# FFN input projection as seven half-size block products per tile pair, with a float32 hidden result and a down projection that walks the depth

## The chip, the cores and the metric

The kernel runs on one core of a Trainium2 chip. The metric is device time in microseconds (us). Five engines of the core work side by side and are ordered only by semaphores: TensorE (PE) multiplies, VectorE (DVE), ScalarE (ACT) and GpSimd (POOL) do the element work, and SyncE (SP) issues the DMAs.

## The reference, cut to what matters

Two transformer-like blocks are computed on a sequence of 512 tokens of width 1024. The change touches only the feed-forward part of the first block:

```python
hffn = modulate(rmsnorm(x, g_norm2[l]), shift2, scale2)
a, u = jnp.split(jnp.einsum('bsd,df->bsf', hffn, w_ffn_in[l]), 2, axis=-1)   # f = 2 * 2816
x = x + gate2[:, None, :] * jnp.einsum('bsf,fd->bsd', jax.nn.silu(a) * u, w_ffn_out[l])
```

All of it is float32. The kernel keeps this precision on PE by splitting each operand into a rounded high part (type F32R) and the remainder, the low part; a product is three matmuls: high times high, high times low, low times high.

## The kernel before, in words

Activations lie with the features on the 128 partitions and the 512 tokens along the free axis. The weights come as a stream of units, 128 x 1024 float32 (512 KB): one unit holds the 8 depth blocks of one output tile of 128 features. Each unit passes a ring of 4 slots: SP loads it into `raw` (`load`, L452), ACT writes the high part `w_hi` (`split_hi`, L598), POOL writes the low part `w_lo` = raw - w_hi (`split_lo`, L534), PE uses it and adds to `unit_used`. `split_hi(u)` waits until unit u-4 has been used, `load(u)` until the low part of unit u-4 is made. The streams of the engines are written out by hand, and each engine works its own stream in order.

The norm ahead of the projection is made in two halves of 256 tokens (HALF): DVE writes the normed half to `tn`, ACT the high part `x_hi`, DVE the low part `x_lo` (`normed_half`, `hi_half`, `low_half`). PE works tile pair 0 (units 0 and 1 of "ff_in") half by half as they come, then units 2 and 3 at full width into PSUM banks of `aux`.

There are 22 tile pairs, a gate tile and an up tile each, 44 units. From pair 2 on PE runs `tiles("ff_in", ...)` (L2470), which calls `tile` (L2117): a tile is 8 depth blocks x 3 matmuls = 24 matmuls of 512 columns, 48 for a pair. For each pair ACT makes silu of the gate tile (`ff_pair`, L833), DVE multiplies it with the up tile out of PSUM into `ht` (`ff_product`, L1517, the product in L1520), ACT writes the high part `h_hi` and DVE the low part `h_lo` (L1524). These two hold the whole hidden result, 22 tiles.

The down projection (`down`, L2472) makes the 8 output tiles one after the other, 22 depth blocks x 3 matmuls each, 528 in all; an output is done every 15 us or so. After each, DVE adds it to `resid` (L1544), ACT writes the high part of the next stage's operand (`next_hi`), DVE its low part (L1559) and sums of squares (L1548 to L1556). The next stage, "gdn_in", starts with depth blocks 0 to 3 of its first tile, then four matmuls for the norm's sums (`two_stats`, L2509 to L2512) that wait for the squares of the last output, then blocks 4 to 7.

Of the kernel before, what the change touches and what calls it, by code (L numbers as in the profile page):

```python
# [33 lines left out]
F32 = mybir.dt.float32  # L34
F32R = mybir.dt.float32r
# [91 lines left out]
def loop(eng, n, counts):  # L127
# [15 lines left out]
    ("ff_in", 44), ("ff_out", 24),  # L143
# [4 lines left out]
    ("first", 182), ("gdn_in", 25), ("mix_out", 6), ("kv", 8), ("xq", 8), ("x_val", 8), ("xo", 4),  # L148
# [6 lines left out]
Q_AT, V_AT = (0, 1, 2, 3, 4, 5, 8, 9), (6, 7, 10, 11, 12, 13, 14, 15)  # L155
LEVELS = 7
# [52 lines left out]
def build_program(nc, dram):  # L209
    ctx = ExitStack()  # L210
    with ctx:
# [46 lines left out]
        def overlay(start, *specs):  # L258
# [44 lines left out]
        (ht, h_hi, h_lo), _ = overlay(  # L303
            over, ("ht", (P, 2, T), F32), ("h_hi", (P, FT, T), F32R), ("h_lo", (P, FT, T), F32R))
# [91 lines left out]
        def sem(name):  # L396
# [54 lines left out]
        def _(sp_):  # L451
# [39 lines left out]
            def load_units(first, end):  # L491
                with sp_.Fori(0, (end - first) // 4) as i:
                    for j in range(4):
                        load(At(first + j, i, 4))

# [20 lines left out]
            load_units(rest, U0["mix_out"] + 4)  # L516
# [16 lines left out]
        def _(pool):  # L533
# [13 lines left out]
            split_units(U0["sb_qk"], U0["gdn_in"])  # L547
# [43 lines left out]
        def _(act):  # L591
# [150 lines left out]
            with loop(act, RET_H, [(own["rv_ready"], 4), (own["tile_done"], 8), (own["oraw_ready"], 4),  # L742
                                   (own["stat_ready"], 1), (own["root_ready"], 1), (own["gate_ready"], 4),
                                   (own["oprod_ready"], 4), (own["orh_ready"], 4)]) as i:
# [13 lines left out]
                def product_hi(e):  # L758
                    own["oprod_ready"].next()
                    own["orh_ready"].own(f(orh[:, e, :], oraw[:, e, :]))  # L760
# [19 lines left out]
            for n in range(KT):  # L780
# [6 lines left out]
                own["merged_f"].next()  # L787
                own["merged_hi"].own(f(m_hi[:, n, :], mt[:, n % 2, :]))
# [13 lines left out]
            def hi_half(k, c):  # L802
                own["normed"].next()
                own["norm_hi"].own(f(x_hi[:, k, c], tn[:, k % 2, c], ACT.Identity,
                                     bias=mod[:, 3 * KT + k:3 * KT + k + 1]))
# [27 lines left out]
            def ff_pair(k, u, n, gate_bank, freed):  # L833
                split_hi(u + AHEAD)
                act.wait_ge(unit_used, (u + 1).val())
                own["gate_ready"].own(f(gate_t[:, n, :], gate_bank, ACT.Silu))
                if freed is not None:
                    nc.scalar.sem_inc(acc_free[freed], 1)
                split_hi(u + 1 + AHEAD)
                own["hidden_f"].next()  # L840
                own["hidden_hi"].own(f(h_hi[:, bass.ds(k, 1), :].rearrange("p a n -> p (a n)"), ht[:, n, :]))

            ff_pair(0, At(U0["ff_in"]), 0, bank(At(0)), 0)
            ff_pair(1, At(U0["ff_in"] + 2), 1, aux[:, T:2 * T], None)
            with loop(act, FT // 2 - 1, [(own["gate_ready"], 2), (own["hidden_f"], 2), (own["hidden_hi"], 2)]) as i:
                for n in range(2):
                    ff_pair(i * 2 + (2 + n), At(U0["ff_in"] + 4 + 2 * n, i, 4), n, bank(At(2 * n)), 0)
            next_hi = {3: 0, 6: 1, 9: 2, 12: 3, 15: 4, 18: 5, 21: 6, 23: 7}
            for j in range(24):
                split_hi(At(U0["ff_out"] + j + AHEAD))  # L850
                if j == 8:
                    own["nega_ready"].own(f(nega[0:GDN_H, 0:1], cols[0:GDN_H, C0["a_log"]:C0["a_log"] + 1], ACT.Exp))
                    nc.scalar.preload_act_table_set("natural_log_exp_and_others")
                if j in next_hi:
                    k = next_hi[j]
                    own["res_ready"].next()
                    own["norm_hi"].own(f(x_hi[:, k, :], resid[:, k, :], scale=gain1[:, k:k + 1]))
# [245 lines left out]
            own["tile_done"].skip(6)  # L1103
# [46 lines left out]
            def hidden_half(n):  # L1150
                own["conv2_ready"].next()
                own["hidden_f"].next()
                own["hidden_hi"].own(f(at_tile(g_hi, n), ht2[:]))
# [15 lines left out]
            with loop(act, FT // 2 - 2, [(own["scaled"], 4), (own["conv0_ready"], 4), (own["conv2_ready"], 4),  # L1169
                                         (own["silu2_ready"], 2), (own["hidden_f"], 2), (own["hidden_hi"], 2)]) as i:  # L1170
# [26 lines left out]
        def _(dve):  # L1197
# [154 lines left out]
            for n in range(PAIRS):  # L1352
                own["gate_ready"].next()
                dve.wait_ge(unit_used, U0["sb_out"] + n + 1)
                own["msb_ready"].own(V.tensor_tensor(msb[:, n, :], sb_bank(n), gates[:, n, :], ALU.mult))
# [37 lines left out]
            with loop(dve, RET_H, [(own["recip_ready"], 1), (own["rs_ready"], 1), (step, 10 + 3 + 6 + 1 + 1 + 16), (own["qk_rot"], 2), (own["ada_used"], 8), (own["ada1_loaded"], 16 * KT),  # L1393
                                   (own["rsc_done"], 1), (own["rsc_ready"], 1), (own["decay_free"], 1),
                                   (own["oraw_ready"], 4), (own["sq_ready"], 1), (own["root_ready"], 1),
                                   (own["gate_ready"], 4), (own["oprod_ready"], 4), (own["orh_ready"], 4),
                                   (own["or_ready"], 4), (own["ada_ready"], 1), (own["tile_done"], 8)]) as i:
# [16 lines left out]
                for e in range(RET_VT):  # L1414
                    own["gate_ready"].next()
                    own["oprod_ready"].own(V.tensor_tensor(oraw[:, e, :], oraw[:, e, :], gate_t[:, e % 2, :], ALU.mult))
                    own["orh_ready"].next()
                    own["or_ready"].own(V.tensor_tensor(orl[:, e, :], oraw[:, e, :], orh[:, e, :].bitcast(F32),
# [1760 lines left out]
```

## Time and profile before

| | us |
|---|---|
| three runs | 2072.86, 2067.62, 2068.59 |
| median | 2068.59 |
| the profiled execution, first to last instruction (span) | 2066.4 |
| ff_in pairs 2 to 21 in it (868.93 to 1086.56) | 217.63 |
| down projection in it (1086.56 to 1207.43) | 120.87 |

Only the span is given for the profiled execution; it lies 2.2 us below the median of the three runs, which count some start and end of the program as well. In the profile, PE is matmul, PEld its weight load, DVE, ACT and POOL the three others. A matmul's recorded duration overlaps the next one, so its price is the distance from one start to the next. "idle ... <-X" is time in which an engine stood still until X let it go on.

### The profile page before, as it was taken

The numbers are of one execution on the slowest core, as the hardware profiler recorded it, in microseconds if no ns is written. First come the engines' busy times: TensorE is split into PE (matmuls) and PEld (weight loads), VectorE is DVE, ScalarE is ACT, GpSimd is POOL, SyncE is SP. The second block draws the span as 40 slices with busy tenths as digits, with TensorE's granted clock in tenths as the row PEclk, the third lists the DMA queues.
The fourth block names the chain that finished last, engine by engine and source line by source line (L and its number), as shares of the span: only waits on it lengthen the run. The fifth ranks groups of instructions, "written<-read, shape, count | busy, mean of one in ns | idle before, by whom it ended". The sixth has DMA issues, their size and how long they took to land.

```text
span 2066.4 us, 29038 instructions
## 1 busy us (share of the span) xinstructions
PE 2027.5 (98%) x10614; PEld 1653.1 (80%) x10614; DVE 915.2 (44%) x1175; ACT 890.3 (43%) x1103; POOL 898.8 (43%) x412
## 2 busy tenths in 40 slices
PE   9999999999999999999999999988999999999999
PEld 5888878787878788888888887767898778888887
DVE  4354434354545454511113346875671267555312
ACT  4476652323232333433232247678653335444321
POOL 3232234342424244444444546768355134444453
PEclk9999999999999999999999999999999999999999
DMA  8121223434333333233333332220244123333331
GB/s 333 60 63 60 62 77 112 143 107 141 108 134 115 132 95 99 82 92 101 94 99 97 107 96 69 81 62 3 83 142 128 35 82 101 93 95 98 101 103 61
DMA packets 56387, 203.84 MB, mean 99 GB/s; under 512 B 6256, under 2 KB 8432, under 8 KB 54896
## 3 DMA queue, kind: packets, MB, share of 16 engines
q1 hardware_dynamic: 56304, 202.70, 30.2%
q8 instruction: 57, 0.93, 0.2%
q14 instruction: 26, 0.21, 0.0%
HBM read 200.57 MB, written 2.10 MB: 98 GB/s over the span
## 4 chain that ended last, share of the span: by engine, by line
PE 75%; issue 8%; DVE 6%; POOL 4%; ACT 4%; DMA 1%; POOLq 0%; DVEq 0%; SPq 0%; ACTq 0%
PE acc L2089 18%; PE acc L2091 17%; PE acc L2090 17%; PE aux L2089 4%; PE aux L2091 4%; PE aux L2090 4%; POOL w_lo L537 3%; PE acc L2393 2%; POOL cfy L562 1%; DVE qkvf L1747 1%; PE aux L2291 1%; DMA ada<-in_ada 1%; PE aux L2286 1%; DVE cfy L1670 1%; PE aux L2304 1%
## 5 line engine op out<-in xcount | busy, mean ns | idle before, releaser
L537 POOL TENSOR_TENSOR w_lo<-raw,w_hi 128x1024 fp32r<-128x1024 f32 x317 | 775.0, 2450 | 1111.8 <-ACT w_hi L596 1110.9
L596 ACT ACTIVATE w_hi<-raw 128x1024 fp32r<-128x1024 f32 x317 | 335.3, 1061 | 541.9 <-PE acc L2091 400.6
L2089 PE MATMUL acc<-x_hi,w_hi 128*128 128x512 f32 (+1 forms) x1336 | 523.3, 392 | 9.6 <-DVEq L1207 4.0
L2091 PE MATMUL acc<-x_hi,w_lo 128*128 128x512 f32 (+1 forms) x1336 | 516.7, 387 | 0.0
L2090 PE MATMUL acc<-x_lo,w_hi 128*128 128x512 f32 (+1 forms) x1336 | 516.5, 387 | 0.0
L2089 PEld LDWEIGHTS acc<-x_hi,w_hi 128*128 128x128 f32 x1336 | 250.9, 188 | 65.9 <-DVEq L1207 6.0
L2091 PEld LDWEIGHTS acc<-x_hi,w_lo 128*128 128x128 f32 x1336 | 250.8, 188 | 51.8
L2090 PEld LDWEIGHTS acc<-x_lo,w_hi 128*128 128x128 f32 x1336 | 251.0, 188 | 49.7 <-issue 0.5
L1520 DVE TENSOR_TENSOR ht<-acc,tn 128x512 f32<-128x512 f32 x21 | 14.5, 692 | 173.8 <-PE acc L2091 171.3
L1249 DVE SCALAR_TENSOR_TENSOR adac<-ada,c_act,adac 128x1024 f32<-128x1024 f32 x28 | 40.4, 1444 | 92.7 <-DMA ada<-in_ada 92.2
L562 POOL TENSOR_TENSOR cfy<-cfy,tn 128x512 f32<-128x512 f32 x51 | 70.0, 1373 | 21.7 <-ACT tn L596 19.1
L2089 PE MATMUL aux<-x_hi,w_hi 128*128 128x512 f32 x192 | 74.9, 390 | 0.8 <-POOL w_lo L537 0.8
L2090 PE MATMUL aux<-x_lo,w_hi 128*128 128x512 f32 x192 | 74.7, 389 | 0.0
L2091 PE MATMUL aux<-x_hi,w_lo 128*128 128x512 f32 x192 | 74.7, 389 | 0.0
L2089 PE MATMUL acc<-h_hi,w_hi 128*128 128x512 f32 x176 | 69.3, 394 | 0.0
L2091 PE MATMUL acc<-h_hi,w_lo 128*128 128x512 f32 x176 | 69.0, 392 | 0.0
L2090 PE MATMUL acc<-h_lo,w_hi 128*128 128x512 f32 x176 | 68.3, 388 | 0.0
L2089 PE MATMUL aux<-w_hi,x_hi 128*128 128x512 f32 x160 | 63.7, 398 | 0.7 <-DVE x_lo L1279 0.7
L2091 PE MATMUL aux<-w_hi,x_lo 128*128 128x512 f32 x160 | 62.4, 390 | 0.0
L2090 PE MATMUL aux<-w_lo,x_hi 128*128 128x512 f32 x160 | 62.3, 389 | 0.0
L596 ACT ACTIVATE tn<-acc 128x512 f32<-128x512 f32 x37 | 22.1, 597 | 84.2 <-PE acc L2091 84.2
L2089 PE MATMUL acc<-g_hi,w_hi 128*128 128x512 f32 (+1 forms) x154 | 58.1, 378 | 0.0
(536 smaller groups left out, 3573.2 us busy)
## 6 DMA issues: line engine op xcount, KB each, us to landing
raw<-in_weights SPq DMA_DIRECT2D x324, 512.0 KB, 3.6
ada<-in_ada SPq DMA_DIRECT2D x32, 512.0 KB, 3.6
ada<-in_ada_first SPq DMA_DIRECT2D x8, 1024.0 KB, 12.3
resid<-in_x SPq DMA_DIRECT2D x2, 1024.0 KB, 6.2
out<-resid SPq DMA_DIRECT2D x16, 128.0 KB, 1.8
decay<-in_tables SPq DMA_DIRECT2D x4, 256.0 KB, 3.6
memf<-in_mem SPq DMA_DIRECT2D x1, 1024.0 KB, 4.9
angles<-in_tables SPq DMA_DIRECT2D x1, 512.0 KB, 5.2
```

The source lines that it names most:

```text
L537: nc.gpsimd.tensor_tensor(lo_home(u), raw[s][:], hi_home(u).bitcast(F32), ALU.subtract).then_inc(lo_ready, 1)
L562: tap_used.own(nc.gpsimd.tensor_tensor(cfy[:, n, :], cfy[:, n, :], product(tap_used.at.c), ALU.add))
L596: return nc.scalar.activation(out, in_, func, **kw)
L1249: return V.scalar_tensor_tensor(dst[:], w, c, dst[:], ALU.mult, ALU.add)
L1670: ins = V.scalar_tensor_tensor(y, x, w, y, ALU.mult, ALU.add)
L1747: ins = V.scalar_tensor_tensor(y[:, d:], bank(t)[:, 0:T - d], w, y[:, d:], ALU.mult, ALU.add)
L2089: M(out, a_hi, b_hi, start=first, stop=False)
L2090: M(out, a_hi, b_lo, start=False, stop=False)
L2091: return M(out, a_lo, b_hi, start=False, stop=last)
L2286: M(zp[h][:, a + w - v:a + w], negone_r[:], part[:, b:b + v], start=False, stop=False, skip_group_check=True)
L2291: m = M(zp[h][:, a:end], negtri_r[:], part[:, a:end], start=False, stop=part is sp_lo[h], skip_group_check=True)
L2393: m = M(bank(t)[:, j * P:T], rv[:, j, e * P:(e + 1) * P], rsc[:, a:a + w], start=j == 0, stop=j == NB - 1)
```

## The change

For pairs 2 to 21 (FAST = 2 pairs stay as they were), the product of a pair is one level of the Strassen-Winograd scheme. The weight's four blocks are (gate or up) x (first or second half of the depth), the activation's four are (half of the depth) x (half of the tokens). Seven products of 512 deep x 256 tokens take the place of eight: 7 x 4 depth blocks x 3 = 84 matmuls of 256 columns a pair instead of 48 of 512.

The scheme needs sums of blocks. For the activations they are made once, from a float32 copy `xf` of the normed input: three go to `t_hi`, `t_lo`, the fourth replaces a quarter of `x_hi`, `x_lo`. For the weights they are made for each pair: DVE forms four sums of 128 x 512 out of `raw` (`first_sums`, `last_sums`), one of them in place of a part of the raw unit; ACT writes their high parts (`split_sums`), DVE one low part (`sum_low`) and POOL another of 128 x 1024. The products' sums are added by DVE (`middle`, `ending`). The hidden result stays in float32 (`hf`).

The down projection goes through the depth with four output tiles at once, twice; the last 6 depth blocks of the second pass go output by output. The hidden tiles are split into high and low parts (`down_hi`, `down_low`) in a ring of 12, twice each. "ff_out" has 22 units instead of 24. Semaphores are merged and renamed to make room. The core of the diff:

```diff
 # stream of SP
+            load_units(rest, ff0 + 8)
+            for n in range(FT - FAST):
+                sp_.wait_ge(S["pair_made"], n + 1)
+                load(At(ff0 + 8 + 2 * n))
+                load(At(ff0 + 9 + 2 * n))
 # stream of POOL, for each pair
+                    split_lo(u)
+                    split_lo(u + 1)
+                    sums_hi.next()
+                    nc.gpsimd.tensor_tensor(wc_lo[n][:, T:3 * T], sum24[:], wc_hi[n][:, T:3 * T].bitcast(F32),
+                                            ALU.subtract).then_inc(sums_lo, 1)
 # stream of ACT
+            def split_diff(u):
+                own["sum_made"].next()
+                split_hi(u)
+            def split_sums(j, n):
+                if j is not None:
+                    act.wait_ge(S["tile_done"], j.val())
+                own["sum_hi"].own(f(wc_hi[n][:, 0:T], sum1[n]))
+                own["pair_made"].next()
+                own["pair_hi"].own(f(wc_hi[n][:, T:3 * T], sum24[:]))
...
+            with loop(act, (FT - FAST) // 2 - 1, [(own["sum_made"], 2), (own["logits_ready"], 2), (own["gate_ready"], 2),
...
                 for n in range(2):
+                    u = At(ff0 + 2 * FAST + 4 + 2 * n, i, 4)
+                    first_product(n)
+                    split_hi(u)
+                    split_diff(u + 1)
+                    fast_gate(n)
+                    split_sums(At(done + 4 * n + 4, i, 8), n)
...
+            for j in range(4, 22):
+                while made < min(2 * j + 6, 2 * FT):
+                    down_hi(made)
+                    made += 1
+                split_hi(At(U0["ff_out"] + j))
+                if j in (12, 14, 16, 18):
+                    next_hi((j - 12) // 2)
+            for j in range(3):
+                split_hi(At(U0["gdn_in"] + j))
+            for k in range(4, KT):
+                next_hi(k)
 # stream of DVE
+            def first_sums(u, n):
+                a, b = raw[u.slot(RING)], raw[(u + 1).slot(RING)]
...
+                step.own(V.tensor_tensor(sum1[n], b[:, 0:T], b[:, T:2 * T], ALU.add))
+                own["sum_made"].own(V.tensor_tensor(b[:, 0:T], a[:, 0:T], b[:, 0:T], ALU.subtract))
+            def last_sums(u, n, again=True):
+                a = raw[u.slot(RING)]
+                if again:
+                    own["pair_split"].next()
+                step.own(V.tensor_tensor(sum24[:, 0:T], sum1[n], a[:, 0:T], ALU.subtract))
+                own["pair_made"].own(V.tensor_tensor(sum24[:, T:2 * T], a[:, T:2 * T], sum24[:, 0:T], ALU.subtract))
+            def operand_low(n):
...
+                own["sum_hi"].next()
+                own["sum_split"].own(V.tensor_tensor(out, xf[:, k:k + HALF_K, c], hi.bitcast(F32), ALU.subtract))
...
+            first_sums(At(ff0 + 4), 0)
+            step.own(V.tensor_tensor(c_act[:, 0:HALF_K], mod[:, 3 * KT + HALF_K:4 * KT], mod[:, 3 * KT:3 * KT + HALF_K],
+                                     ALU.subtract))
+            for k in range(HALF_K):
+                r = xf[:, HALF_K + k, h1]
+                (step if k < HALF_K - 1 else own["sum_made"]).own(
+                    V.scalar_tensor_tensor(r, r, c_act[:, k:k + 1], xf[:, k, h1], ALU.add, ALU.subtract))
+            step.own(V.tensor_tensor(xf[:, 0:HALF_K, h1], xf[:, 0:HALF_K, h1], xf[:, 0:HALF_K, h0], ALU.subtract))
+            for k in range(HALF_K):
+                r = xf[:, k, h0]
+                (step if k < HALF_K - 1 else own["sum_made"]).own(
+                    V.scalar_tensor_tensor(r, r, shift[k], xf[:, HALF_K + k, h1], ALU.add, ALU.add))
+            for k in range(HALF_K):
+                r = xf[:, HALF_K + k, h0]
+                (step if k < HALF_K - 1 else own["sum_made"]).own(
+                    V.scalar_tensor_tensor(r, r, shift[HALF_K + k], xf[:, k, h0], ALU.add, ALU.subtract))
+            last_sums(At(ff0 + 4), 0, again=False)
+            hidden(0, bank(At(1)), gate_t[:, 0, :])
+            for n in range(3):
+                operand_low(n)
+            sum_low(0)
+            operand_low(3)
+            hidden(1, aux[:, 2 * T:3 * T], gate_t[:, 0, :])
+            first_sums(At(ff0 + 6), 1)
+            last_sums(At(ff0 + 6), 1)
+            sum_low(1)
+            def middle(n, k):
...
+                own["bank_free"].own(V.tensor_tensor(parts[:, h0], parts[:, h0], c[:, h0], ALU.add))
+                step.own(V.tensor_tensor(parts[:, h1], parts[:, h0], c[:, h1], ALU.add))
+                own["tile_done"].next()
+                own["bank_free"].own(V.tensor_tensor(
+                    hf[:, bass.ds(k, 1), :].rearrange("p a (b n) -> p (a b) n", b=2),
+                    parts[:, h1].rearrange("p (a n) -> p a n", a=1).broadcast_to([P, 2, T // 2]),
+                    b.rearrange("p (a n) -> p a n", a=2), ALU.add))
+            def ending(n, k):
+                own["tile_done"].next()
+                own["logits_ready"].own(V.tensor_tensor(a[:, h1], parts[:, h0], b[:, h1], ALU.add))
+                hidden(k, at_tile(hf, k), a)
+            with loop(dve, (FT - FAST) // 2 - 1, [(step, 6), (own["oraw_ready"], 2), (own["sum_made"], 2), (own["pair_split"], 2), (own["pair_made"], 2),
...
                 for n in range(2):
+                    u = At(ff0 + 2 * FAST + 4 + 2 * n, i, 4)
+                    first_sums(u, n)
+                    middle(n, i * 2 + (FAST + n))
+                    last_sums(u, n)
+                    ending(n, i * 2 + (FAST + n))
+                    sum_low(n)
...
+            for n in range(4, KT):
+                down_tile(n)
+                down_x(n)
+                if n < KT - 1:
+                    down_squares(n)
 # stream of PE
+            own["sum_split"].next(3)
+            own["sum_split"].skip()
+            with loop(pe, (FT - FAST) // 2, [(own["pair_split"], 2), (own["sum_split"], 2), (own["bank_free"], 4)]) as i:
                 for n in range(2):
+                    pe.wait_ge(S["tile_f"], At(made + 1 + n, i, 2).val())
+                    wa = weights(u)
+                    product(a[:, h0], *wa, 0, "b11", first=True).then_inc(S["tile_done"], 1)
+                    wb = weights(u + 1)
+                    product(c[:, h1], *wb, 0, "t3", first=True)
+                    product(b[:, h0], *wb, 1, "t4", first=True)
+                    own["pair_split"].next()
+                    product(c[:, h0], wc_hi[n], wc_lo[n], 1, "t2").then_inc(S["tile_done"], 1)
+                    own["sum_split"].next()
+                    product(b[:, h1], wc_hi[n], wc_lo[n], 0, "t1").then_inc(S["tile_done"], 1)
+                    own["bank_free"].next()
+                    product(a[:, h0], *wa, 1, "b21").then_inc(unit_used, 2)
+                    own["bank_free"].next()
+                    product(b[:, h1], wc_hi[n], wc_lo[n], 2, "b22").then_inc(S["tile_done"], 1)
```

`product` is 4 depth blocks x 3 matmuls of 256 columns. `hidden` multiplies with silu of the gate tile, `first_product` copies half of the first product out of PSUM, and both loops of ACT and DVE run over 18 of the 20 pairs, 2 at a time. `operand_low` writes a low part of 128 x 1024.

## Rows read from the trace of the kernel before

**Rows 1.** The page: the span, and PE's busy time.

```profile
span 2066.4 us, 29038 instructions
...
PE 2027.5 (98%) x10614; PEld 1653.1 (80%) x10614; DVE 915.2 (44%) x1175; ACT 890.3 (43%) x1103; POOL 898.8 (43%) x412
```

**Rows 2.** Windows: stretch, its length, then busy us (instructions) by engine, PE clock.

```profile
868.93:1086.56 217.63, 217.63 (x961) 180.24 (x960) 27.71 (x40) 67.08 (x80) 95.77 (x40) 1.00 0.31 97
1086.56:1207.43 120.87, 120.87 (x529) 99.16 (x528) 40.84 (x40) 31.97 (x34) 56.23 (x23) 1.00 0.33 101
```

**Rows 3.** Timeline of PE (start, us): first and last of 93 matmuls, 256 columns.

```profile
817.11 0.28 PE L2089 MATMUL aux<-m_hi,w_hi 128*128 128x256 f32 x1
...
827.94 0.28 PE L2091 MATMUL aux<-m_hi,w_lo 128*128 128x256 f32 x1
```

**Rows 4.** Groups by form, DVE, 780 to 1215: busy, mean ns, idle before.

```profile
L1524 DVE TENSOR_TENSOR h_lo<-ht,h_hi 128x512 f32 x20 | 13.9, 694 | 18.6 <-ACT h_hi L596 18.6
L1487 DVE SCALAR_TENSOR_TENSOR tn<-resid,gain,aux 128x256 f32<-128x256 f32 x16 | 7.7, 481 | 1.0 <-ACT aux L596 0.5
...
L1544 DVE SCALAR_TENSOR_TENSOR resid<-acc,mod,resid 128x512 f32<-128x512 f32 x8 | 6.0, 751 | 70.2 <-PE acc L2091 70.2
```

**Rows 5.** Groups by form, ACT, 780 to 1215.

```profile
L596 ACT ACTIVATE w_hi<-raw 128x1024 fp32r<-128x1024 f32 x79 | 83.6, 1060 | 115.3 <-PE acc L2091 103.3 <-ACT h_hi L596 4.4 <-ACT tn L596 4.3
L596 ACT ACTIVATE h_hi<-ht 128x512 f32 x20 | 12.6, 632 | 88.1 <-DVE ht L1520 88.1
...
L596 ACT ACTIVATE x_hi<-resid,gain 128x512 fp32r<-128x512 f32 x8 | 5.7, 707 | 0.0
```

**Rows 6.** Instructions of one line: duration ns min/median/max, first and last start.

```profile
L537 POOL TENSOR_TENSOR w_lo<-raw,w_hi x41: 2389/2394/2400, 866.0 to 1083.2; 128x1024 fp32r<-128x1024 f32 x41
...
L1831 DVE TENSOR_TENSOR xm<-xm,aux x20: 420/420/423, 1385.9 to 1421.3; 128x256 f32<-128x256 f32 x20
...
L1326 DVE TENSOR_TENSOR sp_lo<-sp,sp_hi x16: 1491/1493/1792, 97.9 to 284.5; 128x1280 fp32r<-128x1280 f32 x16
```

**Rows 7.** Timelines of POOL and DVE in the down projection.

```profile
1115.44 2.42 POOL L537 TENSOR_TENSOR w_lo<-raw,w_hi 128x1024 fp32r<-128x1024 f32 x1 [3.06 <-ACT w_hi L596]
1120.93 2.42 POOL L537 TENSOR_TENSOR w_lo<-raw,w_hi 128x1024 fp32r<-128x1024 f32 x1 [3.08 <-ACT w_hi L596]
...
1117.06 0.75 DVE L1544 SCALAR_TENSOR_TENSOR resid<-acc,mod,resid 128x512 f32<-128x512 f32 x1 [9.64 <-PE acc L2091]
...
1121.57 2.33 DVE L1559 SCALAR_TENSOR_TENSOR x_lo<-resid,gain,x_hi 128x512 fp32r<-128x512 f32 x1 [1.40 <-ACT x_hi L596]
```

**Rows 8.** Timelines of DVE and POOL, 101 to 108.

```profile
102.31 1.72 DVE L1326 TENSOR_TENSOR sp_lo<-sp,sp_hi 128x1280 fp32r<-128x1280 f32 x1 [0.68 <-ACT sp_hi L596]
104.06 2.51 DVE L1296 COPY spare<-v_sb 128x512 f32<-128x512 f32 x1
...
103.44 2.84 POOL L537 TENSOR_TENSOR w_lo<-raw,w_hi 128x1024 fp32r<-128x1024 f32 x1 [0.76 <-ACT w_hi L596]
```

**Rows 9.** Timelines of DVE and POOL where the change's setup begins.

```profile
856.65 0.48 DVE L1492 SCALAR_TENSOR_TENSOR x_lo<-tn,mod,x_hi 128x256 fp32r<-128x256 f32 x1 [0.19 <-ACT x_hi L596]
...
857.72 2.40 POOL L537 TENSOR_TENSOR w_lo<-raw,w_hi 128x1024 fp32r<-128x1024 f32 x1 [9.99 <-ACT w_hi L596]
```

**Rows 10.** Timelines of PE and DVE at the end of the down projection.

```profile
1207.43 0.40 PE L2089 MATMUL acc<-x_hi,w_hi 128*128 128x512 f32 x1
...
1210.20 1.02 PE L2509 MATMUL aux<-spare,two_sums 128*128 128x512 f32 x2
...
1207.70 0.75 DVE L1544 SCALAR_TENSOR_TENSOR resid<-acc,mod,resid 128x512 f32<-128x512 f32 x1 [6.89 <-PE acc L2091]
```

**Rows 11.** Windows, as Rows 2, around the clock's fall.

```profile
1421.80:1424.40 2.60, 0.51 (x16) 0.38 (x9) 1.18 (x2) 2.41 (x7) 2.44 (x3) 1.00 0.00 0
1425.00:1435.00 10.00, 8.77 (x74) 8.24 (x70) 5.48 (x10) 7.36 (x11) 9.45 (x8) 0.50 0.01 3
```

**Rows 12.** Timeline of PE: a gap without a fall.

```profile
1351.10 0.50 PE L2089 MATMUL acc<-x_hi,w_hi 128*128 128x512 f32 x1 [2.51 <-DVEq L1207]
```

More of the change, by code:

```diff
@@ L843, in _ @@
-            ff_pair(0, At(U0["ff_in"]), 0, bank(At(0)), 0)
-            ff_pair(1, At(U0["ff_in"] + 2), 1, aux[:, T:2 * T], None)
-            with loop(act, FT // 2 - 1, [(own["gate_ready"], 2), (own["hidden_f"], 2), (own["hidden_hi"], 2)]) as i:
-                for n in range(2):
[L847 to L857, printed above, removed]
+            ff0 = U0["ff_in"]
@@ new lines, in _ @@
+            first_product(0)
+            split_hi(At(U0["ff_out"]))
+            split_hi(At(U0["ff_out"] + 1))
+            fast_gate(0)
+            first_product(1)
+            for x in range(3):
+                down_hi(x)
+            split_hi(At(U0["ff_out"] + 2))
+            split_hi(At(U0["ff_out"] + 3))
+            fast_gate(1)
+            for x in range(3, 10):
+                down_hi(x)
+            own["nega_ready"].own(f(nega[0:GDN_H, 0:1], cols[0:GDN_H, C0["a_log"]:C0["a_log"] + 1], ACT.Exp))
@@ L2412, in _ @@
                 for e in range(RET_VT):
[L2413 removed]
+                    own["tile_split"].next()
                     project(0, e)
@@ new lines, in product @@
+            def product(out, wh, wl, at_, name, first=False):
+                hi, lo = operand(name)
+                for k in range(HALF_K):
+                    a = slice(at_ * T + k * P, at_ * T + (k + 1) * P)
+                    M(out, wh[:, a], hi[:, k, :], start=first and k == 0, stop=False, skip_group_check=True)
+                    M(out, wh[:, a], lo[:, k, :], start=False, stop=False, skip_group_check=True)
+                    m = M(out, wl[:, a], hi[:, k, :], start=False, stop=k == HALF_K - 1, skip_group_check=True)
+                return m
@@ new lines, in _ @@
+            d0 = U0["ff_out"]
+            for r in range(2):
+                for k in range(FT if r == 0 else FT - 6):
+                    x = r * FT + k
+                    own["tile_split"].next()
+                    if k % 2 == 0:
+                        wh, wl = weights(At(d0 + 11 * r + k // 2))
+                    for n in range(4):
+                        m = down_part(x, 4 * r + n, wh, wl, k % 2 * 4 + n, k == FT - 1, used=n == 1 and x > 0)
+                        if k % 2 and n == 3:
+                            m.then_inc(unit_used, 1)
+                        elif k == FT - 1:
+                            m.then_inc(S["tile_done"], 1)
@@ L3006, in _ @@
                         if n == 0 and k >= FT - 2:
-                            own["hidden"].next()
+                            own["tile_split"].next()
                         at_ = n % 4 * FT + k
```

328 lines of the change are left out of this document (226 added, 102 removed).

## The prediction

> **What bounds the kernel now.** I read the page first: PE is busy for 2027.5 of 2066.4 us, every other engine under half of it [rows 1]. So time can only be won by giving PE less, and any new wait of PE is lost time. The windows say what the stage touched is worth: pairs 2 to 21 take 217.63 us with PE never idle, 960 matmuls of 512 columns, so 226.7 ns each and 10.88 us a pair; POOL is busy for 96 us of it, DVE for 28. The down projection takes 120.87 us for 528 matmuls, also without a gap [rows 2]. Next I looked for matmuls of 256 columns, because the change lives by them: 93 stand in a row in the output projection, 92 distances in 10.83 us, 117.7 ns each, with waits that are already met between them [rows 3]. Last, and this decides the forecast, I compared the timelines of DVE and POOL. POOL's low part takes 2.39 us alone [rows 6]. A DVE operation with a PSUM operand runs through beside it in its usual 0.75 us. One whose two inputs both lie in SBUF started at 1121.57 while POOL ran to 1123.35 and ended at 1123.90: it stood still until POOL was done and took 0.55 us more [rows 7]. It works the other way too. POOL, called at 103.44 during such a DVE operation, took 2.84 us, and the next DVE operation, called 0.03 us after the first had ended, waited 2.2 us for POOL [rows 8]: whoever already waits goes first, so the two take turns.
>
> The Trainium skill states this as a rule ("SBUF — State Buffer", section "Who interferes with whom"): the port pair that DVE and GpSimd share is an exclusive lock, taken by a DVE instruction with two SBUF inputs against a GpSimd instruction that reads SBUF, and the loser waits. The trace agrees, by the rows named. It speaks against this change.
>
> **The pair, what PE gains.** 84 matmuls x 117.7 ns = 9.89 us instead of 10.88, so 0.99 us a pair and 19.8 us for 20 pairs. That is all the change can win. (The Trainium skill, "TensorE: Matmul & The Clock Gate", section "Wait — 56ns, not 53.3ns?", gives columns divided by 2.4 GHz plus 2.5 ns; by it a pair would go from 10.35 to 9.17 us, a gain of 1.18. The trace shows about 11 ns on top in place of 2.5, and I go by the trace.)
>
> **The pair, what is laid on the others.** POOL gets three operations of 1024 columns instead of two: 3 x 2.39 = 7.2 us. ACT gets three of 1.06, two of about 0.6 and a copy, 4.8 us [rows 5], no limit. DVE gets ten: five with a PSUM operand, which no one disturbs (0.42 us for 256 columns [rows 6], 0.69 for 512 [rows 4]), and five with both inputs in SBUF (`first_sums` 2, `last_sums` 2, `sum_low` 1), which share the lock with POOL: 0.69 us each, 0.55 after a wait. Together the lock is held 7.2 + 5 x 0.55 to 0.69 = 10.0 to 10.6 us a pair, already more than PE's 9.89. The order makes it worse, since one of these operations stands ahead of what PE waits for.
>
> I walk one pair j of the loop, from time 0, the end of the pair before. Hand-offs are 0.1 to 0.3 us (DVE starts 0.27 us after the nominal end of the last matmul [rows 10]). ACT's `split_hi` could start when product b21 of the pair before was done, at -1.2, and ends at -0.1. POOL: first low part 0 to 2.4. DVE adds the last product (0.2 to 0.6), ACT makes silu behind its second weight split (to 1.6) and the high part of the sum (to 2.3), DVE multiplies (to 2.45). `sum_low` is called at 2.5, when POOL has just started its second low part (2.3 to 4.7), and ends at 5.25. POOL's third, called since about 3.5, goes 5.2 to 7.55. `first_sums` is called at 5.3, between them: its first half waits to 7.55 and ends at 8.1, its second runs 8.15 to 8.85. Only then does DVE reach `middle`, whose data were there at 5.9 (four products, 5.65 us): 8.9 to 9.3. PE finished its fifth product at 7.06 and waits for `bank_free` until 9.45. The two products left end at 12.3; the other two additions of `middle` fit beside the sixth. So a pair takes 12.3 us, not 9.9: 1.42 us more than before, although PE works less. If `sum_low` gets in before the second low part, the same walk gives 12.1. `last_sums` falls into POOL's pause (10.6 to 12.1) and costs nothing, and the loads have over 5 us of air.
>
> **The first pairs.** Operand sums and splits stand between the last `low_half` (ends at 857.13 [rows 9]) and the third product, and PE waits for three of them before pair 2 begins, which before began at 868.93. DVE's list: two sums of 512 (1.4), a tiny one, 12 of 256 columns at 0.48 plus the gap between two [rows 4], one of 1024, two of 512, `hidden(0)` 0.7, three low parts of 1024. For 1024 columns I take 1.22, on the line between 0.69 at 512 and 1.49 at 1280 [rows 4, 6]. Alone that is 15.1 us, to 872.2, so 3.3 us of waiting. But POOL has five operations in this stretch (low parts of units 3 to 6 and the new one), and nearly all of DVE's are of the locked kind. Taking turns: unit 3 from 857.9 to 860.3 makes the second sum end at 860.85; units 4 and 5 follow, the first `xf` sum ends at 866.1, the chain of `xf` sums at 873.2, `hidden(0)` at 875.4, then low part, POOL, low part, POOL, low part: 876.7, 880.2, 883.6. PE starts pair 2 at 883.75: +14.8 us. Behind this DVE still has `sum_low(0)`, the fourth low part, `hidden(1)`, four sums for pair 3, `sum_low(1)` and the sums for pair 4 before `middle` of pair 2, with POOL twice between: `middle` starts at 895.8 and pair 2 ends at 899.2, 15.45 us instead of 10.88: +4.6.
>
> **The rest of the pairs.** Pairs 3 to 19 at 12.3: 17 x 1.42 = +24.2. The last two have no sums to make for later pairs: 9.9 and 10.2, together -1.7.
>
> **Down projection.** The same 528 matmuls. DVE's 44 low parts (0.69) and POOL's 22 (2.4) fit: two and one in every 24 matmuls, 5.44 us, with 6 tiles or 16 us of lead. Cover gone would show as waits on `tile_split`; I set nothing. The dropped empty units cost nothing before either.
>
> **Start of the next stage.** Outputs 4 to 7 now end 18 matmuls, 4.1 us, apart, instead of 15. ACT's stream has `split_hi` of gdn_in unit 2 ahead of `next_hi(4)`, and that waits for ff_out unit 20, used 8 x 3 matmuls = 5.4 us before the end. So with the last matmul's nominal end as 0, `next_hi(4)` ends at -3.4; DVE, which waits for it with all else queued behind, writes x_lo(4) after POOL at -1.1. Then 2.2 us of squares, and for each output 0.75 [rows 4], 0.71 on ACT [rows 5] with hand-offs 0.3, 0.75, 2.2: 4.7 us. Output 7's square on ACT is ready at 13.1. PE is at `two_stats` after 2.77 us [rows 10]: +10.3.
>
> **The clock.** PE's granted clock fell to 0.50 (1.2 GHz) once, after 2.6 us with 0.51 us of work, and stood there for some 10 us though PE was busy for 8.8 of them [rows 11]; after a gap of 2.51 us with work on both sides it did not fall [rows 12]. The two long gaps here (14.8 and 10.3 us) should each bring a fall. Ten us at half speed cost at most 5 us; at the first gap most is hidden behind the wait for `middle`. Bounds 0 to 10, I take 4. The gaps of 2.3 us in each pair are shorter than the one without a fall, so nothing there.
>
> **Sum.** 14.8 + 4.6 + 24.2 - 1.7 + 10.3 + 4 = 56.2 us: span 2066.4 to 2122.6, median 2068.59 to 2124.8.
>
> **The rivals.** (1) *The lock does not decide*, and PE sets the pace of the pairs: -19.8 for the pairs, +3.3 at their start, +10.3 at the next stage, +0 to 4 for the clock: 2062 to 2066, not slower. It decides as soon as POOL and DVE together hold the lock for less than PE's 9.89 us, or `middle` does not stand behind `first_sums` while POOL works. Against it speak [rows 7, 8], for it only that DVE is idle for most of the stage today. 10%. (2) *POOL does not get in between two DVE operations that follow at once*: `sum_low` and `first_sums` then run through to 6.7, a pair takes 10.2, the twenty 204 us instead of 217.6. With 3.3 to 14.8 at the start, 10.3 and the clock: 2070 to 2086. The timeline of [rows 8] speaks against it. 12%. (3) *The clock falls in the gaps of the loop.* Ten us low in a pair cost 5.1 us of work, so such a pair takes 15.0 us; every second one: +24, each one: +49; 2149 to 2174. 8%. (4) *Not what it says*: the seven products are there in the code and 84 x 256 against 48 x 512 columns is certain, so I give this nothing.
>
> **The numbers.** My case has 70%, with 2105 to 2140 for its own range (12.1 to 12.6 a pair, 5 us either way at each gap, the clock's bounds). To hold 8 in 10 the range goes down to 2082, into rival 2, and ends at 2140. A measurement of this kernel tells some 0.3% (6 us) from no change. Faster: half of rival 1, 5%. Same: the rest of it and the lowest of rival 2, 9%. Slower 86%.
>
> **What would show it.** In the loop, PE idle some 2.3 us a pair on DVE's `bank_free`, ahead of the sixth product; `first_sums` at 2.3 to 2.8 us where it meets POOL, and DVE operations out of PSUM at 0.42 and 0.69 as ever; POOL's operations end to start in threes. Pair 2 starting near 884 and a pair every 12.3 us. At gdn_in, `two_stats` 13 us after the last down matmul. The forecast is wrong if PE's idle time in the loop is nil, if `first_sums` runs in the gap before POOL's third operation, or if pair 2 starts near 872.

## The result, and the profile after

The changed kernel takes 2134.45 us (median of 4 runs, 2126.09 to 2135.82) beside 2070.7 us for the kernel before on the same chip: ratio 1.0304, 95% interval 1.0283 to 1.0326. Forecast were 2124.8 us, from 2082 to 2140. The profiled execution has a span of 2132.6 us, 66.2 more than before. The page of it, its span and part 1:

```profile
span 2132.6 us, 31113 instructions
## 1 busy us (share of the span) xinstructions
PE 2037.6 (96%) x11334; PEld 1692.8 (79%) x11334; DVE 1146.2 (54%) x1395; ACT 944.3 (44%) x1187; POOL 956.3 (45%) x430
```

PE's busy time rose by 10 us although its work in this stage fell by some 19 (twenty pairs at 9.95 us, the pace of an experiment below, for 217.63) [rows 1, 2]; I come back to that under the clock. The rest is waiting, and the view of PE's waits from 855 to 1285 us names every place (waiting line, releaser: us in total, times, longest):

```profile
PE aux L2744 <- DVE tn L1731: 34.4, 18, 3.7
PE aux L2744 <- DVE t_lo L1683: 14.0, 1, 14.0
PE aux L2814 <- ACT sqt L648: 9.7, 1, 9.7
```

L1731 is the first addition of `middle`, L1683 is `operand_low`, L648 is any ACT operation, here output 7's square. Three places, as forecast. The windows of the pairs and of the down projection (columns as in rows 2):

```profile
883.03:1138.97 255.94, 221.50 (x1680) 217.77 (x1681) 195.67 (x199) 92.27 (x121) 149.58 (x58) 0.92 0.26 82
1138.97:1262.18 123.21, 123.21 (x531) 99.80 (x529) 75.71 (x70) 55.31 (x72) 59.27 (x23) 1.00 0.30 95
```

The twenty pairs take 12.80 us each instead of 10.88. DVE, at 28 us before, is now busy for 196 us of 256, and PE's clock is no longer 1.00 but 0.92 [rows 2]. One turn of the loop on the timelines of DVE and POOL shows the mechanism:

```profile
962.18 0.43 DVE L1743 TENSOR_TENSOR aux<-tn,aux 128x256 f32<-128x256 f32 x1 [1.89 <-PE aux L2746]
963.26 0.69 DVE L1687 TENSOR_TENSOR hf<-hf,aux 128x512 f32 x1 [0.65 <-ACT aux L648]
964.07 2.85 DVE L1677 TENSOR_TENSOR wc_lo<-tn,wc_hi 128x512 fp32r<-128x512 f32 x1
967.40 2.33 DVE L1664 TENSOR_TENSOR spare<-raw 128x512 f32<-128x512 f32 x1 [0.48 <-DVE wc_lo L1677]
969.76 0.69 DVE L1665 TENSOR_TENSOR raw<-raw,raw 128x512 f32<-128x512 f32 x1
970.67 0.42 DVE L1731 TENSOR_TENSOR tn<-tn,aux 128x256 f32<-128x256 f32 x1 [0.22 <-DVE raw L1665]
...
961.59 4.78 POOL L576 TENSOR_TENSOR w_lo<-raw,w_hi 128x1024 fp32r<-128x1024 f32 x2 [5.31 <-ACT w_hi L648]
966.32 2.86 POOL L595 TENSOR_TENSOR wc_lo<-sum,wc_hi 128x1024 fp32r<-128x1024 f32 x1
```

`sum_low` (L1677) is called at 964.07 and ends at 966.92, 0.55 us after POOL's second operation (966.37). POOL's third (L595) was called in the meantime and, taking 2.86 instead of 2.39 us, runs to 969.18. The first half of `first_sums` (L1664) is called at 967.40, and ends at 969.73, again 0.55 us after POOL. Only then do its second half and `middle` come. The operations with `aux` from PSUM keep their 0.43 and 0.69 us in the midst of POOL's work. PE in the same turns:

```profile
920.47 0.39 PE L2744 MATMUL aux<-x_hi,w_hi 128*128 128x256 f32 x1 [1.93 <-DVE tn L1731]
932.59 0.39 PE L2744 MATMUL aux<-x_hi,w_hi 128*128 128x256 f32 x1 [1.92 <-DVE tn L1731]
...
957.51 0.56 PE L2744 MATMUL aux<-x_hi,w_hi 128*128 128x256 f32 x1 [1.92 <-DVE tn L1731]
971.15 0.55 PE L2744 MATMUL aux<-x_hi,w_hi 128*128 128x256 f32 x1 [1.92 <-DVE tn L1731]
971.50 0.42 PE L2745 MATMUL aux<-x_lo,w_hi 128*128 128x256 f32 x1
971.71 0.41 PE L2746 MATMUL aux<-x_hi,w_lo 128*128 128x256 f32 x1
984.77 0.52 PE L2744 MATMUL aux<-x_hi,w_hi 128*128 128x256 f32 x1 [1.91 <-DVE tn L1731]
```

PE waits ahead of the sixth product in 18 of the 20 pairs: 3.70 us in pair 2, then some 1.92 us, and 1.1 to 1.9 in pairs behind a fall of the clock. The distance from one such wait to the next is 12.12 us where the clock stays up (920.47 to 932.59) and 13.6 us from 957.51 on, where it falls: the matmuls behind the wait follow each other at 0.21 us instead of 0.12.

### The profile page after: what moved, and what is told of

The parts are those of the page before. It is cut to its first block, busy times and chain, and to the rows that moved or that the text cites. A ratio compares the mean times of both kernels' runs of the same rounds, so it can differ in the third digit from the quotient of the medians.

```text
span 2132.6 us, 31113 instructions
## 1 busy us (share of the span) xinstructions
PE 2037.6 (96%) x11334; PEld 1692.8 (79%) x11334; DVE 1146.2 (54%) x1395; ACT 944.3 (44%) x1187; POOL 956.3 (45%) x430
## 4 chain that ended last, share of the span: by engine, by line
PE 32%; DVE 10%; issue 9%; ACT 4%; POOL 4%; DVEq 0%; ACTq 0%; POOLq 0%
PE acc L2347 4%; PE acc L2349 4%; PE acc L2348 4%; POOL w_lo L576 3%; PE aux L2347 2%; PE aux L2349 2%; PE aux L2348 2%; DVE wc_lo L1677 2%; PE aux L2744 1%; PE aux L2777 1%; PE aux L2778 1%; PE aux L2774 1%; DVE raw L1665 1%; DVE tn L1664 1%; PE aux L2746 1%
## 5 line engine op out<-in xcount | busy, mean ns | idle before, releaser
L648 ACT ACTIVATE w_hi<-raw 128x1024 fp32r<-128x1024 f32 x315 | 330.9, 1059 | 616.3 <-PE acc L2349 313.2
L2347 PE MATMUL acc<-x_hi,w_hi 128*128 128x512 f32 (+1 forms) x1016 | 399.5, 393 | 7.8 <-DVEq L1346 3.6
L2349 PE MATMUL acc<-x_hi,w_lo 128*128 128x512 f32 (+1 forms) x1016 | 393.0, 387 | 0.0
L2348 PE MATMUL acc<-x_lo,w_hi 128*128 128x512 f32 (+1 forms) x1016 | 392.7, 386 | 0.0
L2347 PEld LDWEIGHTS acc<-x_hi,w_hi 128*128 128x128 f32 x1016 | 191.3, 188 | 51.9 <-DVEq L1346 5.7
L2349 PEld LDWEIGHTS acc<-x_hi,w_lo 128*128 128x128 f32 x1016 | 191.1, 188 | 39.5
L2348 PEld LDWEIGHTS acc<-x_lo,w_hi 128*128 128x128 f32 x1016 | 191.4, 188 | 37.4 <-issue 0.5
L2744 PE MATMUL aux<-x_hi,w_hi 128*128 128x256 f32 x160 | 52.7, 329 | 48.4 <-DVE tn L1731 34.4
L595 POOL TENSOR_TENSOR wc_lo<-sum,wc_hi 128x1024 fp32r<-128x1024 f32 x20 | 56.9, 2843 | 9.7 <-ACT wc_hi L648 9.7
L2349 PE MATMUL acc<-g_hi,w_lo 128*128 128x512 f32 (+1 forms) x154 | 57.9, 376 | 0.0
L2348 PE MATMUL acc<-g_lo,w_hi 128*128 128x512 f32 (+1 forms) x154 | 57.4, 373 | 0.0
```

Of the source, the lines that this page charges most:

```text
L595: nc.gpsimd.tensor_tensor(wc_lo[n][:, T:3 * T], sum24[:], wc_hi[n][:, T:3 * T].bitcast(F32), ALU.subtract).then_inc(sums_lo, 1)
L648: return nc.scalar.activation(out, in_, func, **kw)
L2347: M(out, a_hi, b_hi, start=first, stop=False)
L2348: M(out, a_hi, b_lo, start=False, stop=False)
L2349: return M(out, a_lo, b_hi, start=False, stop=last)
L2744: M(out, wh[:, a], hi[:, k, :], start=first and k == 0, stop=False, skip_group_check=True)
```

## The experiments

Spans of single executions differ by up to 6 us ahead of this stage, so places are compared by distances inside the stage. The measure used is the time from PE's fourth wait for `x_lo` in pair 0 (the mark) to the start of `two_stats`, on PE's timeline (of before and of after; before's `two_stats` is in [rows 10]):

```profile
850.29 0.38 PE L2089 MATMUL acc<-x_hi,w_hi 128*128 128x256 f32 x1 [0.54 <-DVE x_lo L1492]
...
850.22 0.39 PE L2347 MATMUL acc<-x_hi,w_hi 128*128 128x256 f32 x1 [0.54 <-DVE x_lo L1631]
...
1274.75 2.07 PE L2814 MATMUL aux<-spare,two_sums 128*128 128x512 f32 x2 [9.65 <-ACT sqt L648]
```

359.9 us before and 424.5 after, so 64.6 of the 66.2 us.

**e1_middle_first.** In DVE's loop, nothing else:

```diff
-                    first_sums(u, n)
                     middle(n, i * 2 + (FAST + n))
+                    first_sums(u, n)
                     last_sums(u, n)
```

> One swap on DVE against the changed kernel: in the loop middle(j) runs before first_sums. Nothing is taken away; all operations of DVE and POOL stay. If it is the order on DVE together with the shared lock (theory): first_sums, when it meets POOL, no longer stands ahead of bank_free, PE's wait of 1.9 us a pair goes, a pair takes 9.9 to 10.1 us, the clock stays at full in the loop, and the 17 periods shrink from 219 to about 170: span 2132.6 to about 2084. If POOL's and DVE's sum of lock time is the bound whatever the order (10.0 to 10.6 us a pair): 2086 to 2096, with PE waiting elsewhere. If the wait has nothing to do with what stands ahead of middle: no change, 2130 to 2134.

Measured: 2106.34 us, ratio 1.0183 (1.0159 to 1.0207); inside the stage -30.2 us, the pairs at 11.28 us. The order matters, but the span, 2102.2 us, lies 6 us above the higher of the two forecasts. The waits on L1731 are still there, 15.9 us in 15 cases, and the timelines of one of them (DVE, POOL, ACT, PE) show where they moved:

```profile
917.33 2.81 DVE L1672 TENSOR_TENSOR sum<-spare,raw 128x512 f32<-128x512 f32 x1
920.18 2.77 DVE L1673 TENSOR_TENSOR sum<-raw,sum 128x512 f32<-128x512 f32 x1
923.07 0.43 DVE L1743 TENSOR_TENSOR aux<-tn,aux 128x256 f32<-128x256 f32 x1
...
917.19 5.21 POOL L576 TENSOR_TENSOR w_lo<-raw,w_hi 128x1024 fp32r<-128x1024 f32 x2 [1.65 <-ACT w_hi L648]
...
926.14 0.38 ACT L648 ACTIVATE tn<-aux 128x256 f32<-128x256 f32 x1
...
927.03 0.57 PE L2744 MATMUL aux<-x_hi,w_hi 128*128 128x256 f32 x1 [2.52 <-DVE tn L1731]
```

Now it is `last_sums` (L1672, L1673) that alternates with POOL's two operations, 5.6 us instead of 1.4. Behind it stand `ending` (L1743), ACT's `fast_gate` and `split_sums`, and behind these on ACT the copy `tn<-aux` that `middle` of the next pair needs. The window of the pairs:

```profile
883.61:1109.28 225.67, 209.69 (x1680) 206.55 (x1681) 170.88 (x199) 94.61 (x121) 151.79 (x58) 0.96 0.28 93
```

DVE is busy for 171 us in the pairs instead of 196, so its meetings with POOL cost it less than before, but they have not gone: now they hold up what stands behind `last_sums`. The clock still falls, which the expectation had left out (0.96).

**e2_pool_64_columns and e8_pool_512_columns.** In POOL's loop the three `tensor_tensor` get 64 (e8: 512) of 1024 columns; the rest of these low parts is left out, the waits and signals stay:

```diff
-                    split_lo(u)
-                    split_lo(u + 1)
+                    for v in (u, u + 1):
+                        s = v.slot(RING)
+                        pool.wait_ge(hi_ready, (v + 1).val())
+                        nc.gpsimd.tensor_tensor(w_lo[s][:, 0:64], raw[s][:, 0:64], w_hi[s][:, 0:64].bitcast(F32), ...
```

> POOL's three operations of each fast pair write 64 columns instead of 1024 (the rest of these low parts is left out, so the output is not the reference's); DVE's order is that of the changed kernel. Two operations of 960 columns on POOL are added once in the setup. Lock theory: with the lock held only for a fraction of a us, first_sums takes 0.69 us every time, middle starts when its product is done, PE's wait of 1.9 us a pair is gone although DVE does the same work in the same order, a pair takes 9.9 to 10.1 us; span 2080 to 2088. Rival, DVE itself is too slow for its place (its ten operations and their waits are the chain): a pair stays at 12.1 or more and the span above 2120.

> Edit: as e2, but POOL's three operations of the loop have 512 columns, not 64 (the rest of the low parts is left out, so the output is not the reference's). This asks from which size on the lock decides. The lock is then held 3 x 1.2 + 5 x 0.55 to 0.69 = 6.4 to 7.0 us a pair, under PE's 9.9, and first_sums can meet at most 1.2 us of POOL twice ahead of middle, which has 1.4 us of air: no wait in the loop, and the span as e2's to 5 us (2077 to 2082), clock 1.00 in the loop. Rival (any meeting costs PE its length): 2 x 1.2 us a pair at least for a part of the pairs, 2095 or more.

Measured: 2078.81 and 2084.09 us (one run each). The windows 895 to 1080 of e2 and then of e8:

```profile
895.00:1080.00 185.00, 184.95 (x1565) 184.75 (x1564) 113.63 (x182) 84.49 (x112) 22.77 (x54) 1.00 0.32 107
...
895.00:1080.00 185.00, 184.58 (x1560) 184.38 (x1560) 131.24 (x184) 85.56 (x113) 75.17 (x56) 1.00 0.32 103
```

DVE's and PE's instructions and their order are those of the changed kernel, and inside the pairs PE has no wait left in e2 and one of 0.42 us in e8: 10.04 and 10.11 us a pair instead of 12.80, pair 2 with its slow start included, 9.93 in the others but the last. That shows POOL's long operations as the cause of the waits, and that at half of its columns the pair is already PE's. (That it is the lock, and not what else depends on POOL's speed, is left to e9.) The falls of the clock go with the waits: without them it stays at 1.00. The spans, 2077.0 and 2082.3 us, lie 3 us under the one forecast and at the upper end of the other.

**e3_next_stage_order.** On ACT `next_hi(4)` and `next_hi(5)` ahead of the splits of gdn_in units 1 and 2; on DVE, for outputs 4 to 7:

```diff
-                down_x(n)
                 if n < KT - 1:
                     down_squares(n)
+                down_x(n)
```

> Only the start of the next stage: ACT makes next_hi(4) before the weight splits of gdn_in units 1 and 2 and next_hi(5) before that of unit 2, and DVE takes the squares of an output before it waits for the high part. Theory: each output then costs DVE about 3.9 us, under the 4.1 to 4.2 between outputs, two_stats begins about 3 us after the last down matmul instead of 12.6, the clock does not fall: 9.8 us of wait and 1.5 us of slow two_stats go, span 2132.6 to 2121 to 2123. Rival, POOL's low parts hold DVE's squares as well and the backlog stays: under 5 us gained, 2128 or more.

Measured: 2123.16 us, ratio 1.0247 (1.0218 to 1.0277), so -11.3 us on the median. PE's wait ahead of `two_stats` is

```profile
1264.45 1.16 PE L2817 MATMUL aux<-spare,two_sums 128*128 128x512 f32 x2 [2.05 <-ACT sqt L648]
```

2.05 us where the changed kernel has 9.65. The order of ACT's and DVE's queues made 7.6 us of that wait, and the time is the one the theory gave.

**e4_setup_order.** On DVE `last_sums(At(ff0 + 4), 0, again=False)` goes behind the three `operand_low` for which PE waits.

> Only the setup: last_sums for pair 2 moves behind the three low parts that PE waits for, so POOL's new low part of this pair comes behind them too. Theory: two sums (1.4 us), one POOL operation (2.4) and the one behind it are taken from the chain ahead of PE, pair 2 starts 4 to 6 us earlier, at 877 to 879 instead of 883.0, and its third to fourth product finds its weights ready; span 2126 to 2129. Rival, what follows pair 2 on DVE (its middle stood behind sums for pairs 3 and 4) eats it: pair 2 starts earlier but its sixth product still begins at 893 to 895.3, span 2131 or more.

Measured: 2135.13 us (one run). PE's timeline:

```profile
883.77 0.57 PE L2744 MATMUL aux<-x_hi,w_hi 128*128 128x256 f32 x1 [8.56 <-DVE t_lo L1683]
892.01 0.39 PE L2744 MATMUL aux<-x_hi,wc_hi 128*128 128x256 f32 x1 [0.97 <-DVE x_lo L1683]
902.52 0.58 PE L2744 MATMUL aux<-x_hi,w_hi 128*128 128x256 f32 x1 [8.85 <-DVE tn L1731]
```

The first wait is 5.4 us shorter, and the next two take it all back: 18.4 us in three waits here, 17.7 in two (13.98 and 3.70) in the changed kernel. This execution reached the mark at 856.38. Counted from there pair 2 begins 5.4 us earlier, but its sixth product begins 1.0 us later and it ends 1.6 us later than in the changed kernel. Advancing one item of an overfull list moves the wait, it doesn't remove it: the rival was right about the place. The total can't tell it, since two kinds of chance are in it: this execution came to the stage 6.2 us later, and the stage was 5.8 us shorter even so, with 8 falls of the clock in the pairs instead of 12.

**e5_18_pairs.** `FAST = 4`: pairs 2 and 3 are plain. DVE's list is put in a new order with it: the operand sums and three `operand_low` come ahead of the sums of the first two fast pairs, with `hidden(0)` to `hidden(3)` spread between them.

> Edit: pairs 2 and 3 are made plainly too (18 pairs by seven products instead of 20), so that DVE's operand sums and splits lie beside 22 us of matmuls. Nothing else is changed. Theory (the wait ahead of the first fast pair is DVE's list, held up by POOL): the wait of 13.98 us goes, the 4.5 us of pair 2 over a plain pair's 10.88 go, and pair 3 costs 10.88 instead of 12.9: -20.5 us, median 2114. Rival (the list is so long that it ends late even so, or the first fast pair then waits for the sums as pair 2 did): up to 14 us of it come back, 2115 to 2128.

Measured: 2112.91 us, ratio 1.023 (1.0194 to 1.0266), inside the stage -20.0 us against the changed kernel. Pair 4 begins without a wait at 891.54, 40.4 us after the mark, as in the kernel before. In its place PE waits 1.35 us for `x_lo` and 3.51 us for `middle` in that first pair, since DVE's sums still meet POOL there. The theory held, with a small part of the rival.

**e6_18_pairs_reordered.** e5 with e1's and e3's edits.

> Edit: e5's, with DVE's middle ahead of first_sums (as in e1) and the order at the start of the next stage (as in e3). Theory: the three do not overlap, so the sum of the parts: 2134.5 - 20.5 - 27 (30 us for 20 pairs in e1, so 27 for 18) - 11 = 2076. Rival (the reordering gained from the same wait as the late start): 2085 or more.

Measured: 2087.01 us, ratio 1.0091 (1.0075 to 1.0106), so the rival's side. The pairs take 11.36 us, 13 waits on `middle` with 14.7 us. The stage lost 51.5 us; the parts measured singly (20.0 for e5, 27.2 for e1 at 18 pairs, 14.5 for e3) sum to 61.7. What overlaps is probably the clock. It falls 12 times in the pairs of the changed kernel, 4 times in e1, 8 times in e3 and in e5, and 4 times in e6: singly the parts took away 16 falls, together 8. At 1.3 to 1.5 us each (below) that is 10 to 12 us, and 10.2 are missing.

**e7_sums_in_psum.** e6, with the sums that DVE reads again in the two PSUM banks of `acc` that are empty in this stage, and the second sum's low part made by DVE instead of POOL. Both pairs in work now share one buffer for the first sum, ACT makes three high parts, and PE waits for POOL's part only ahead of the last product. The core of the edit:

```diff
-        sum1 = [spare[:], tn[:, 1, :]]
+        sum1, sum2, sum4 = acc[:, 0:T], acc[:, T:2 * T], sum24[:, T:2 * T]
-                    nc.gpsimd.tensor_tensor(wc_lo[n][:, T:3 * T], sum24[:], wc_hi[n][:, T:3 * T].bitcast(F32), ...
+                    nc.gpsimd.tensor_tensor(wc_lo[n][:, 2 * T:3 * T], sum4, wc_hi[n][:, 2 * T:3 * T].bitcast(F32), ...
```

> Edit: e6's, and the two sums that DVE reads again are written into the two PSUM banks that stand empty in this stage (spare banks of acc), and the low part of the second is made by DVE out of PSUM, so POOL's third operation has 512 columns instead of 1024. DVE gets one operation more, but only 2 of them have two SBUF inputs. Lock theory: the lock is held 2 x 2.39 + 1.2 + 2 x 0.69 = 7.4 us a pair, less than PE's 9.9, so PE sets the pace, 18 pairs at 9.95 where e6 takes some 11.3: -24 us, median 2052 (2050 to 2058), faster than the kernel before. Rival (DVE's number of operations sets the pace, not the lock): the pair takes as long as in e6 or longer, 2076 to 2090.

Measured: 2059.34 us (median of 5) beside 2067.88, ratio 0.9957 (0.9943 to 0.997): faster than both kernels, by 0.4% against the one before. The theory's pace (9.95) came true; its range (2050 to 2058) was missed by 1.3 us, because it was reckoned from 2076 for e6, which took 2087. The window of its 18 pairs, and DVE and POOL in one of them:

```profile
893.68:1072.78 179.10, 179.05 (x1514) 178.85 (x1513) 120.25 (x191) 88.00 (x127) 105.19 (x54) 1.00 0.32 106
...
972.79 0.70 DVE L1687 TENSOR_TENSOR acc<-acc,raw 128x512 f32<-128x512 f32 x1
973.52 0.69 DVE L1688 TENSOR_TENSOR sum<-raw,acc 128x512 f32<-128x512 f32 x1
...
973.06 4.78 POOL L577 TENSOR_TENSOR w_lo<-raw,w_hi 128x1024 fp32r<-128x1024 f32 x2 [3.89 <-ACT w_hi L649]
```

9.95 us a pair, no wait and the clock at 1.00, with DVE doing one operation more. `last_sums` (L1687, L1688) runs in 0.70 and 0.69 us while POOL is at work from 973.06 to 977.84.

**e9_sums_in_sbuf.** e7 with one line changed:

```diff
-        sum1, sum2, sum4 = acc[:, 0:T], acc[:, T:2 * T], sum24[:, T:2 * T]
+        sum1, sum2, sum4 = spare[:], sum24[:, 0:T], sum24[:, T:2 * T]
```

> Edit: e7's kernel with one line changed: the two sums lie in SBUF again (spare and the first half of sum24), not in PSUM. The number, order and size of all instructions are e7's. Theory (what e7 gained came from DVE operations that, with one PSUM operand, no longer share the lock with POOL): six operations of DVE have two SBUF inputs again, the lock is held 4.78 + 1.3 + 6 x 0.55 to 0.69 = 9.4 to 10.2 us a pair, about PE's 9.9, so waits come back in a part of the pairs: pairs at 10.2 to 11.0 instead of e7's 9.95, +5 to +19 us, 2064 to 2078. Rival (e7's gain came from POOL's smaller operation and the shorter hand-offs alone): as e7 within 3 us, 2059.

Measured: 2094.23 us, ratio 1.0114 (1.0094 to 1.0133) against e7's 0.9957. The same two operations:

```profile
974.96 2.74 DVE L1687 TENSOR_TENSOR sum<-spare,raw 128x512 f32<-128x512 f32 x1
977.73 2.78 DVE L1688 TENSOR_TENSOR sum<-raw,sum 128x512 f32<-128x512 f32 x1
...
974.75 5.22 POOL L577 TENSOR_TENSOR w_lo<-raw,w_hi 128x1024 fp32r<-128x1024 f32 x2 [2.81 <-ACT w_hi L649]
```

Pairs at 11.64 us instead of 9.95. Instructions, sizes and order are e7's, so the rule is shown directly: it is the second SBUF input that makes these additions of DVE wait for POOL. The pace is no better than e6's 11.36, so POOL's smaller operation and the changed hand-offs gained nothing by themselves: the rival is out. The window of the 18 pairs:

```profile
891.44:1100.97 209.53, 189.94 (x1513) 186.98 (x1512) 168.42 (x195) 89.85 (x127) 120.64 (x53) 0.96 0.27 90
```

The loss is larger than I expected, for two reasons. I took the sum of lock times (9.4 to 10.2 us) for the cost, but in four of the pairs both halves of `last_sums` meet POOL, 4.1 us at once, with ACT's copy for the next `middle` behind them, and PE waits 2.7 us there, 17.2 us in all. And the clock falls again (0.96), which I had not reckoned with: of the 30 us lost against e7's pairs some 8 are its own. The Trainium skill ("SBUF — State Buffer", section "Who interferes with whom") says that a DVE instruction with at most one SBUF input, outside the modes that use both ports, does not contend with GpSimd. e7 and e9 agree for `tensor_tensor`, 0.70 against 2.74 us for the same operation. One SBUF input alone is not enough, though: the operation that waited in [rows 8] is a copy with a single input, from SBUF to SBUF, and the eight of its kind in the kernel before take

```profile
L1296 DVE COPY spare<-v_sb x8: 427/2507/2510, 104.1 to 286.0; 128x512 f32<-128x512 f32 x8
```

0.43 us once, with POOL idle, and 2.51 us the other seven times, beside POOL.

## Why the prediction was right, step by step

Against the profile before, in us:

| step | forecast | measured |
|---|---|---|
| wait ahead of pair 2 | +14.8 | +14.1 (883.03 for 868.93) |
| 17 periods of the loop, lock alone | +24.2 | +21.1 (12.12 for 10.88) |
| clock falls in these periods | 0 | +13.0 |
| pair 2 and the last two | +2.9 | +4.2 |
| down projection | 0 | +2.3 |
| wait ahead of `two_stats` | +10.3 | +9.8 |
| clock at both long gaps | +4 | +1.5 at the second; the first is inside pair 2 |
| sum | +56.2 | +66.0 |

- *Gain of PE*: 84 matmuls in 9.89 us. e7's pairs take 9.95, e2's 9.93 behind pair 2. Right.
- *The lock and its turns*: right, in mechanism and size. The pace without a fall of the clock is 12.12 us where I had walked to 12.3 or 12.1, the wait 1.92 where I had 2.3. The order of the turns is the one walked to 12.3: `sum_low` waits for POOL's second operation, the first half of `first_sums` for its third, and `middle` comes behind both. It is only a little earlier, 8.7 us after the pair's first matmul instead of 8.9. One row that the walk leaned on needs a word: the DVE operation that let POOL in between in [rows 8] is a copy with one SBUF input, not an addition with two. That additions take turns in the same way is shown by the turn above.
- *The setup*: `operand_low` ended at 882.70, forecast 883.6. e5 shows the place (the wait goes when DVE has two more pairs of time and its list in a new order); that it is a full list and not one item of it, e4 shows.
- *"Nothing for the clock" in the gaps of the loop*: wrong, and the largest miss, 13 us. It failed where I took one gap of 2.51 us without a fall [rows 12] as a bound for gaps that come back in every pair. The windows right behind the wait of 1.92 us at 971.15 and in a pair without a fall:

```profile
971.20:972.00 0.80, 0.80 (x4) 0.80 (x5) 0.55 (x2) 0.00 (x0) 0.00 (x0) 0.51 0.00 0
...
951.00:953.00 2.00, 2.00 (x20) 2.00 (x19) 1.97 (x2) 0.92 (x2) 2.00 (x1) 1.00 0.63 168
```

  Ten times in the 17 periods the clock stood at half, for 3.0 to 3.6 us, and such a period took 12.8 to 13.6 us, 1.3 us more on average (13.0 / 10). This is rival 3, at a smaller price than I gave it: I had carried over the 10 us of the fall in [rows 11] and came to 24 or 49 us. The falls are also the main reason why PE's busy time rose though its work fell: 221.5 us in the window of the pairs, for 20 x 9.95 = 199 us of work at e7's pace.
- *Down projection*: PE has no wait there, as forecast, but its matmuls come every 233.3 ns instead of 228.9, also in the last 72, which go bank by bank as before. So neither waits nor the changing of banks make it. The cause stays open.
- *Next stage*: right, by order as by size; e3 took 7.6 us of the wait away. e3's distance inside the stage is 14.5 us shorter. The rest, 7.0 us, lies in the pairs, where its code is that of the changed kernel: 8 falls of the clock for 12 (0.94 for 0.92) and a first wait for `middle` of 2.3 us for 3.7. I put that down to chance.
- *Rivals 1 and 2*: fallen. For rival 1 the condition held in e2, e7 and e8, where POOL or the number of locked operations was cut, and there the pairs were PE's.

The total came out right in part by luck. The sum was 10 us short: it had nothing for the 13 us of the clock in the loop, and 3 us too much in its other terms together. That stayed within the range only because the range had been left wide for the pace of the pairs and for the two long gaps, which hardly missed. Had a fall cost what rival 3 said, the time would have lain beyond 2140.

## What to carry to other kernels

Before giving DVE new work beside a busy POOL, count its operations with two SBUF inputs, and its copies from SBUF to SBUF: each that meets POOL costs up to POOL's whole operation, and what stands behind it on DVE and ACT pays as well. Look first where PE's release stands in that queue, then put one input of these additions in an idle PSUM bank; here that one line was worth 1.6% (ratio 1.0114 to 0.9957). A cheaper algorithm also has a setup: let the first items go the plain way until its operands are ready, which was worth 20 of the 65 us here.

## What the runs showed of the hardware

- In the changed kernel, behind gaps of 1.8 to 1.9 us that come back each pair (once of 3.7 us), PE's clock fell to half in some of the pairs and not in others, at once or up to 1.2 us after the gap, for 3.0 to 3.6 us each time. In e1 the same gap of 2.52 us brought a fall in three of five cases, and the one of 2.51 us before none [rows 12]. Without gaps (e2, e7) there was none behind the first pair. Such a short fall costs 1.3 to 1.5 us, nearly as much as the gap itself. What decides whether it comes stays open.
- A DVE addition of 512 columns that waited for POOL ends 0.55 us after POOL's operation, and takes 0.69 us alone; a POOL operation of 1024 columns called while DVE held the lock shows 2.86 us instead of 2.39. With one input in PSUM such an addition takes 0.70 us in the midst of POOL's work.
- Matmuls of 512 columns in the same formats came at 226.7 ns in the FFN's input projection, 228.9 in the down projection before and 233.3 in it after, at full clock.
